# Samples' attention in nine wide products, and products that nobody reads in four waits of the first head pair

## What is computed

```python
def swa_sample(q, k, v, cache_k, cache_v, sinks, table):   # Bn = 8 requests, L = 4 tokens
    keys = concatenate([cache_k, k], axis=1)                # 128 cached + 4 new
    vals = concatenate([cache_v, v], axis=1)
    logits = einsum('bqhgd,bkhd->bhgqk', qh, keys) * HEAD_DIM ** -0.5
    ...
    probs = sink_softmax(logits + head_bias(dist, table), mask, s)
    out = einsum('bhgqk,bkhd->bqhgd', probs, vals)
```

## Time and profile before

| what | value |
| --- | --- |
| three runs | 2802.87, 2808.48, 2809.76 us (median 2808.48) |
| the profiled execution's own time | 2807.99 us |
| its span | 2806.2 us |
| mean granted TensorE clock | 0.956 of full |
| busy share | PE 94%, PEld 88%, DVE 58%, ACT 33%, POOL 11% |
| chain that ended last | PE 78%, DVE 10%, issue 5%, ACT 5% |

### The profile page before, as it was taken

The page is one execution under the profiler, slowest core; times in us unless marked ns, Lnnn a source line. Parts: engine busy times, 40 slices in busy tenths (PEclk is TensorE's granted clock), DMA queues, the critical chain, the costliest instruction groups (busy, mean ns, idle before and its releaser), DMA issues.

```text
span 2806.2 us, 59577 instructions
## 1 busy us (share of the span) xinstructions
PE 2629.9 (94%) x23314; PEld 2456.8 (88%) x23314; DVE 1630.7 (58%) x2395; ACT 927.5 (33%) x1681; POOL 297.4 (11%) x324
## 2 busy tenths in 40 slices
PE   8999999978888999999999999998788889999997
PEld 8999999866666899999899999997666678999996
DVE  5666436665566566663366653467556646666534
ACT  4333223442222333332243332343322214333323
POOL 1030110003510100001100001100214101000011
PEclk9999999988988999999999999999789989999997
DMA  3853234310001223223222222441000022223221
GB/s 111 98 98 89 84 90 126 95 33 5 10 10 54 69 82 89 85 85 91 78 83 86 86 86 87 121 113 47 29 1 10 10 80 64 86 87 88 83 88 58
DMA packets 380503, 201.69 MB, mean 72 GB/s; under 512 B 41461, under 2 KB 376821, under 8 KB 379528
## 3 DMA queue, kind: packets, MB, share of 16 engines
q1 hardware_dynamic: 377928, 197.46, 24.4%
q0 software_dynamic: 2400, 1.82, 2.0%
HBM read 188.07 MB, written 13.34 MB: 72 GB/s over the span
## 4 chain that ended last, share of the span: by engine, by line
PE 78%; DVE 10%; issue 5%; ACT 5%; SPq 1%; DMA 1%; DVEq 0%; POOLq 0%; ACTq 0%; POOL 0%
PE ps L690 56%; PE ps L745 21%; DVE ar L1962 3%; ACT ar L1452 2%; DVE ar L1956 2%; SPq L537 1%; ACT wh L1380 1%; DVE wl L1840 1%; DVE x L1956 1%; PE ps L1033 0%; DVE ar L1992 0%; DVE xl L1947 0%; DMA raws<-in_w_in 0%; DMA ar<-in_x_sample 0%; ACT L1732 0%
## 5 line engine op out<-in xcount | busy, mean ns | idle before, releaser
L1840 DVE TENSOR_TENSOR wl<-raws,wh 128x1024 fp32r<-128x1024 f32 x336 | 411.1, 1224 | 670.3 <-ACT wh L1380 666.0
L690 PE MATMUL ps<-xh,wh 128*128 128x272 f32 x2880 | 605.8, 292 | 14.8 <-DVE wl L1840 12.2
L690 PE MATMUL ps<-xh,wl 128*128 128x272 f32 x2880 | 600.3, 290 | 0.0
L690 PE MATMUL ps<-xl,wh 128*128 128x272 f32 x2880 | 598.9, 289 | 0.0
L745 PE MATMUL ps<-ar 64*64 64x64 f32 (+12 forms) x5484 | 437.9, 270 | 97.0 <-ACT ar L1452 37.2
L1380 ACT ACTIVATE wh<-raws 128x1024 fp32r<-128x1024 f32 x336 | 354.7, 1057 | 414.4 <-PE ps L690 378.3
L745 PEld LDWEIGHTS ps<-ar 64*64 64x64 f32 (+5 forms) x5484 | 315.3, 155 | 194.3 <-issue 55.2
L690 PEld LDWEIGHTS ps<-xh,wh 128*128 128x128 f32 x2880 | 458.4, 191 | 18.5 <-DVE wl L1840 14.8
L690 PEld LDWEIGHTS ps<-xl,wh 128*128 128x128 f32 x2880 | 458.5, 190 | 0.0
L690 PEld LDWEIGHTS ps<-xh,wl 128*128 128x128 f32 x2880 | 457.7, 190 | 0.0
L690 PE MATMUL ps<-hh,wh 128*128 128x272 f32 x1408 | 292.2, 289 | 0.0
(11 more groups left out here) (199 smaller groups left out, 2762.7 us busy)
## 6 DMA issues: line engine op xcount, KB each, us to landing
raws<-in_ffn_w_in SPq DMA_DIRECT2D x176, 512.0 KB, 3.7
raws<-in_ffn_w_out SPq DMA_DIRECT2D x64, 512.0 KB, 3.4
raws<-in_w_in SPq DMA_DIRECT2D x42, 512.0 KB, 3.7
raws<-in_ffn_w_out SPq DMA_DIRECT2D x32, 384.0 KB, 3.0
raws<-in_w_out SPq DMA_DIRECT2D x16, 448.0 KB, 3.6
x_kept<-x SPq DMA_DIRECT2D x2, 2176.0 KB, 10.1
x<-x_kept SPq DMA_DIRECT2D x2, 2176.0 KB, 8.0
ar<-in_consts SPq DMA_DIRECT2D x2, 1337.5 KB, 6.6
```

The source lines that it names most:

```text
L690: ins = pe.matmul(ps[:, bank + h, 0:n1 - h * NH], w[u % 2][:, k, :], a[:, k0 + k, h * NH:n1], start=(first and k == 0 and n == 0), stop=(l ...
L1840: dve.tensor_tensor(wl[u % 2][:, :, :], raw[u % 2][:, :, :], wh[u % 2][:, :, :].bitcast(F32), ALU.subtract).then_inc(sem("wl_done"), 1)
```

## The change

Two things, both in the first part of the mixing stage.

First, the samples' attention output. The 8 transposes of the new values become one of 128x32, so that the 32 new values stand on 32 partitions (`vn`, 32x128) instead of 4 partitions times 8 requests. VectorE gets one more operation: `att_x`, the probabilities on the 4 new keys spread over all 8 requests and multiplied by the new constant `own`, which is zero for other requests. The transposes of line 886 then read `att_x` (128x32). The output is made by one product of `vn` with all 256 probability columns, and one product for each request with both key-value heads at once: weights 128x128, 32 moving columns. Half of each result is not used. VectorE's four copies read the half that belongs to them.

Second, pair 0 gets `unread(2)` at four places: before the wait for `lora` (with two waits of the samples moved ahead of it), between the second and third `cum` product before the wait for `kk_read`, after `cum` before the wait for `dec`, and after `bonus_sum` before the wait for `prep`. The last but one stood there for the other pairs already.

```diff
-                    for b in range(DEC_BATCH):
-                        ins = pe.transpose(ps[0:DEC_SEQ, 6 + b // 4, b % 4 * P:(b % 4 + 1) * P], proj[:, V_CH, SEQ + 4 * b:SEQ + 4 * b + 4], ident)
-                    ins.then_inc(*tick("probs_t"))
+                    pe.transpose(ps[0:NSAMP, 6, 0:P], proj[:, V_CH, SEQ:NT], ident).then_inc(*tick("probs_t"))
...
                     for j in range(2):
                         pe.transpose(ps[:, 6, j * P:(j + 1) * P], att_s[:, j, 0:P], ident)
-                        ins = pe.transpose(ps[0:DEC_SEQ, 7, j * P:(j + 1) * P], att_s[:, j, P:NKEY_S], ident)
+                    pe.wait_ge(sem("probs"), at(lay, "probs", HALVES + 2))
+                    for j in range(2):
+                        ins = pe.transpose(ps[0:NSAMP, 7, j * P:(j + 1) * P], att_x[:, j, :], ident)
...
-                    for j in range(2):
-                        for b in range(DEC_BATCH):
-                            o = j * P + 16 * b
-                            mm(ps[0:HD, 4, o:o + 16], cv[:, b, j * HD:(j + 1) * HD], pts[:, o:o + 16], stop=False)
-                            ins = mm(ps[0:HD, 4, o:o + 16], vn[:, b, j * HD:(j + 1) * HD], ptn[:, o:o + 16], start=False)
+                    both = [t.rearrange("p (j n) -> p j n", j=2) for t in (ps[:, 4, 0:2 * P], pts)]
+                    mm(ps[:, 4, 0:2 * P], vn, ptn, stop=False, skip_group_check=True)
+                    for b in range(DEC_BATCH):
+                        out_b, pts_b = (t[:, :, 16 * b:16 * b + 16] for t in both)
+                        ins = mm(out_b, cv[:, b, :], pts_b, start=False, stop=(b == DEC_BATCH - 1), skip_group_check=True)
                     ins.then_inc(*tick("attn"))
...
                     if q == 0:
+                        pe.wait_ge(sem("y_copied"), at(lay, "y_copied", HALVES))
+                        pe.sem_inc(passed, 1)
+                        pe.wait_ge(sem("pt_v"), at(lay, "pt_v", HALVES))
+                        unread(2)
                         pe.wait_ge(sem("lora"), at(lay, "lora", 1))
...
                         if i == 2:
+                            if q == 0:
+                                unread(2)
                             pe.wait_ge(sem("kk_read"), at(lay, "kk_read", q + 1))
...
-                    if q:
-                        unread(2)
+                    unread(2)
                     yield
                     pe.wait_ge(sem("dec"), at(lay, "dec", q + 1))
...
                     blk_sum(U[:, TMP, :], 2, "bonus_sum")
+                    if q == 0:
+                        unread(2)
...
-                    for h in range(2):
-                        go(vn[:, 4 * h:4 * h + 4, :].rearrange("p b d -> p (b d)"), ps[0:DEC_SEQ, 6 + h, :]).then_inc(*tick("pts"))
+                    go(vn, ps[0:NSAMP, 6, 0:P]).then_inc(*tick("pts"))
...
                     normalise(att_s, 2, HALVES + 1, stats_s)
+                    dve.wait_ge(sem("probs"), at(lay, "probs", HALVES + 1))
+                    tt(att_x.rearrange("p j (b t) -> p j b t", b=DEC_BATCH),
+                       bc(att_s[:, :, P:NKEY_S].rearrange("p j (o t) -> p j o t", o=1), [P, 2, DEC_BATCH, DEC_SEQ]),
+                       bc(cst("own").rearrange("p (o b u) -> p o b u", o=1, u=1), [P, 2, DEC_BATCH, DEC_SEQ]), ALU.mult).then_inc(*tick("probs"))
...
-                    pv = ps[0:HD, 4, 0:2 * P].rearrange("p (j b g t) -> p j g b t", j=2, b=DEC_BATCH, g=4)
                     for j in range(2):
+                        pv = ps[j * HD:(j + 1) * HD, 4, j * P:(j + 1) * P].rearrange("p (b g t) -> p g b t", b=DEC_BATCH, g=4)
```

More of the change, by code:

```diff
@@ L69 @@
          ("umask1", HD), ("rw_s", 3 * NSAMP + DEC_BATCH), ("neg_incl_s", NSAMP), ("gmask_s", 4 * NSAMP),
-         ("lmask_s", len(S_LEVELS) * NSAMP), ("umask1_s", NSAMP), ("sel", 2 * P), ("rowmask", DEC_BATCH),
+         ("lmask_s", len(S_LEVELS) * NSAMP), ("umask1_s", NSAMP), ("sel", 2 * P), ("rowmask", DEC_BATCH), ("own", DEC_BATCH),
          ("id64", HD), ("onehot", 3 * P)]
@@ L123, in constants @@
     put("rowmask", own)
+    put("own", (i // (4 * DEC_SEQ))[:, None] == np.arange(DEC_BATCH)[None])
     n = 2 * P - 1 - np.arange(3 * P)
@@ L256 @@
                   "m0_t": 2, "m_next": 16, "neg_max": 9, "newton_end": 8, "par_in": 352, "cv_in": 16, "par_early": 208, "prep": 4,
-                  "probs": 9, "probs_t": 10, "pt_a": 6, "pt_v": 8, "pts": 4, "qk_sq": 4, "qk_sum": 4, "qm": 11,
+                  "probs": 10, "probs_t": 10, "pt_a": 6, "pt_v": 8, "pts": 3, "qk_sq": 4, "qk_sum": 4, "qm": 11,
                   "qm_zero": 1, "rows_s": 2, "rows_t": 1, "rs_exp": 4, "s0_copied": 8, "s0_t": 2,
@@ L388, in trunk @@
         assert _o <= M_NORM
-        vn, _o = region(M_NORM, DEC_BATCH * P)
+        vn, _o = region(M_NORM, P)
+        att_x, _o = region(_o, 2 * NSAMP)
         assert _o <= M_NORM + 2 * NT
@@ L412, in trunk @@
         vt = vt.rearrange("p (i d) -> p i d", i=TILES)
-        vn = vn[0:DEC_SEQ].rearrange("p (b d) -> p b d", b=DEC_BATCH)
-        ptn = ptn[0:DEC_SEQ]
+        vn = vn[0:NSAMP]
+        att_x = att_x.rearrange("p (j n) -> p j n", j=2)
+        ptn = ptn[0:NSAMP]
         ys = ys.rearrange("p (c n) -> p c n", c=4)
@@ L879, in samples_attend @@
                     yield
-                    pe.wait_ge(sem("pts"), at(lay, "pts", 2))
+                    pe.wait_ge(sem("pts"), at(lay, "pts", 1))
                     pe.sem_inc(passed, 1)
                     pe.wait_ge(sem("probs"), at(lay, "probs", HALVES + 1))
-                    pe.sem_inc(passed, 1)
                     for j in range(2):
                         pe.transpose(ps[:, 6, j * P:(j + 1) * P], att_s[:, j, 0:P], ident)
-                        ins = pe.transpose(ps[0:DEC_SEQ, 7, j * P:(j + 1) * P], att_s[:, j, P:NKEY_S], ident)
+                    pe.wait_ge(sem("probs"), at(lay, "probs", HALVES + 2))
+                    for j in range(2):
+                        ins = pe.transpose(ps[0:NSAMP, 7, j * P:(j + 1) * P], att_x[:, j, :], ident)
                     ins.then_inc(*tick("probs_t"))
                     yield
-                    pe.wait_ge(sem("pts"), at(lay, "pts", 4))
+                    pe.wait_ge(sem("pts"), at(lay, "pts", 3))
                     pe.sem_inc(passed, 1)
@@ L1542, in samples_attend @@
                     go(pts, ps[:, 6, 0:2 * P]).then_inc(*tick("pts"))
-                    go(ptn, ps[0:DEC_SEQ, 7, 0:2 * P]).then_inc(*tick("pts"))
+                    go(ptn, ps[0:NSAMP, 7, 0:2 * P]).then_inc(*tick("pts"))
                     yield
@@ L2104, in samples_attend @@
                     dve.wait_ge(sem("attn"), at(lay, "attn", HALVES + 1))
-                    pv = ps[0:HD, 4, 0:2 * P].rearrange("p (j b g t) -> p j g b t", j=2, b=DEC_BATCH, g=4)
                     for j in range(2):
+                        pv = ps[j * HD:(j + 1) * HD, 4, j * P:(j + 1) * P].rearrange("p (b g t) -> p g b t", b=DEC_BATCH, g=4)
                         for p in range(2):
                             dve.tensor_copy(ys[64 * p:64 * p + 64, 2 * j:2 * j + 2, :].rearrange("p c (b t) -> p c b t", b=DEC_BATCH),
-                                            pv[:, j, p:p + 3:2, :, :]).then_inc(*tick("ys"))
+                                            pv[:, p:p + 3:2, :, :]).then_inc(*tick("ys"))
                     yield
```

## The result

The changed kernel takes 2776.69 us, the median of 7 runs (2763.70 to 2790.30). The kernel before, timed beside it, has a median of 2809.76 us in 7 runs (2802.87 to 2818.50). The ratio is 0.9883, with a 95% interval of 0.9864 to 0.9902: faster by 1.2%, 33 us, where I forecast 23 us (2786, range 2777 to 2800). The profiled execution took 2776.02 us (span 2774.2), so rows and median tell of the same time.

A forecast was written before the change was run, and what follows sets the result against it. TensorE was taken as the bound, 78% of the chain, with the clock at 0.76 in the changed stretch. Terms 6.0 + 4.05 + 1.4 = 11.45 us a layer, 22.9 for two, gave 2786 us; range 2777 to 2800.

The forecast's parts named there:

- a sum of 11.45: Saving a layer in us: 6.0 from wide products, 4.05 from unread products, 1.4 from the inverse after them.
- Up to the Gram products: Pair 0, from the stage's start to the first Gram product: unread products hold the clock and save 4.05 us a layer.
- the 0.5 us: Pair 0's first products at full clock, after the first unread place: ACT's chain and what hangs on it come 0.5 us earlier.
- the second wait: Pair 0's wait before `kk_read`: 4.7 us long, 2.8 left empty, so the clock falls and the records after it gain 0.
- the cap by the output queue: ACT's first token copy waits for the last output DMA, so the Gram products come at most 4.0 us earlier.
- The products: Samples' output: 18 wide records in about 2.4 us replace 64 taking 8.40, saving 6.0 us a layer, between 4.3 and 7.3.
- After them: Inverse behind the samples' output: the clock stays up, saving 1.3 us for the slow level, 1.4 with the piece after.
- Rival A: The clock is not held, only the wide products pay: 0.5 + 5.6 us a layer, 2795.8 us; chance 0.30.
- Rival B: Unread products run at half clock on the path, sticking out by 4.2 us a layer: 2808 us, no change; chance 0.07.
- Rival C: Slower: low clock phases return in the 301 us after the stretch, 2834 us at clock 0.85; chance 0.05.
- my own signs of being wrong: Wide records over 0.2 us, scores' clock at 0.5, an unread product starting after its wait's end, or the 301 us growing.
- Part 3: What follows the samples' output: the inverse gains 1.4 us a layer, the rest of the stage does not change.

The follow-up runs named there:

- experiments 7: Changed kernel with the cached values in 16 narrow products writing alternating output halves, and no unread products at the second place: 2781.40 us, ratio 0.9922.
- 9: Changed kernel with 32 more TensorE semaphore increments a layer that nobody waits for, behind the second unread place: 2792.91 us, ratio 0.9939.
- experiment 1: Changed kernel without pair 0's four places of unread products, the wide products kept: 2786.93 us, ratio 0.9921 against the kernel before.
- 10: Changed kernel with 16 more TensorE semaphore increments a layer that nobody waits for, behind the second unread place: 2771.66 us, ratio 0.9879.

## Why the prediction missed by nine microseconds

**The part that I worked out came true.** A layer's stretch fell from 78.5 to 67.1 us, 11.4 us, against a sum of 11.45.

- Up to the Gram products, in layer 0: 32.8 to 29.1 us, so 3.7 against 4.05. The first products took 1.51 us instead of 1.94, but of the 0.5 us only 0.2 arrive at the `g_mm` products (19.8 to 19.6 us after the start). From there to the transposes 5.97 us became 4.85, 1.1 as forecast. Transposes and scores took 2.80 us instead of 5.13, up to the start of the next transposes, 2.3 against 2.5. The clock fell in the second wait as expected (0.69), and the cap by the output queue held.
- The products: 8.40 to 2.60 us, 5.8 against 6.0. The 128x32 records took 0.125 us each; I had taken 0.12. The Trainium skill, "TensorE: Matmul & The Clock Gate", section "LDWEIGHTS (loading the stationary operand)", by which the part would save 1.5 us, is not borne out: its 1.9 us for the new loads lies near the 2.60 us measured, its 3.4 us for the old ones far from 8.40. What makes them dear, by the record starts above, is the change of rows at every product, and that no two products in a row write different halves.
- After them: 15.82 to 14.04 us, 1.8 against 1.4. The next level took 3.69 us at full clock instead of 5.17, and the rest of the inverse gained 0.3 us more.

Between the Gram products and the output 0.1 us was lost, so layer 0 alone gives 11.1. That the terms together come so near to 11.45 is in part luck: two terms were too large and one too small, and in experiments 7 and 9 one more low phase came with a stretch some 3 us longer.

Rival A fell with the clock of the stretch, 0.95 and 0.92 with the unread products against 0.77 and 0.81 without (experiment 1, whose median of 2786.93 is itself less than the 2795.8 that I gave A). Rival B fell with the timeline: the first pair of unread products ran at full clock, and the waits after them stayed open. Rival C, the low phases coming back, was named for the right place, but for both layers together it went the other way. One of my own signs of being wrong did show: the 301 us after the stretch grew in layer 0, to 305.75.

**The step that failed** is in Part 3: "Of the rest of the stage (301 us to 983.00) I expect no change", with its reason that the times are 300.98 and 300.40 us at clocks of 0.93 and 0.88, "so where the low phases fall matters by less than 1 us". The second time was cut 11.2 us short. The real pair, 301.88 and 311.30 us, says the opposite: nearly the same work, 9.4 us apart. It was also one execution, and the repeats show the spread. So I priced at nothing a term that came out at about 4.5 us a layer, 9 us for both, where the median came out 9.3 us below the forecast; that the two agree so closely is luck. Over the profiled executions, 22.9 us from the stretches and 9 from the rest, less 2.7 us by which everything else grew (2036.0 and 2033.5 us before, 2037.7 and 2037.3 after), make 29, the mean of the two pairs (32.0 and 26.5). The medians, with more runs, differ by 33; the 4 us between lie within what single executions vary.

**Why the rest got shorter** is settled in part. Shown: of the 9 us in both layers some 3 are idle time and some 6 a lower clock for the same records; 1.9 us a layer lie in one segment of pair 1 and repeat; and 16 more TensorE instructions ahead of the rest move the median by 21 us while the work stays. By their count all fourteen rests fall into a short and a long group, and the change, with 74 fewer, goes from the long to the short one. Not settled: why the border lies between 24 and 32 more, and how the count leads to low phases of the clock. The issue waits differ too little between 9 and 10 to show it, and the segment of pair 1 did not go back to 79.9 us in both layers when 74 instructions were put back. That it is the place in the instruction stream, and not the moment at which the rest begins, is argued and not shown. None of the variants is shown to beat the change. The 2771.66 us of the 16 increments has a ratio of 0.9879, within the interval of the change itself.

## What to carry to other kernels

Price a stretch that follows a change by several executions, and let its instruction count confirm the cut: a window with 3178 records beside one with 3226 is a different window. On TensorE, let small products in a row write alternating halves of the output's partitions, and keep products of the same number of rows together, before you make them wide. After a change that adds or removes tens of TensorE instructions, try two or three harmless shifts before judging a gain of half a per cent: here a shift alone was worth 0.8%.

## What the chip showed that I had not expected

- Records of 128x64 weights and 16 columns took 0.034 us each when the output halves alternated. Two of them start 0.007 us apart in different halves, and 0.079 us apart in one product. A change between weights of 128 and of 4 or 32 rows took 0.134 to 0.140 us.
- One semaphore increment on TensorE took 0.11 us (74 in 8.10 us).
- One kernel's executions spread over 26.6 us: the shortest (2763.70) had a mean granted clock of 0.973, the longest (2790.30) 0.960. In its rows the same work took 296.3 us at 0.93 and 306.9 at 0.89.
